# Sample attention: fetching the value pages from GpSimd's queue instead of the sync engine's

## What is computed

```python
k_past = cache_k[i][page_table].reshape(bs, past, SB_HEADS, SB_HEAD_DIM)
v_past = cache_v[i][page_table].reshape(bs, past, SB_HEADS, SB_HEAD_DIM)
...
z = jnp.einsum('bqhd,bkhd->bhqk', qblk, k) * scale + bias
log_1mb = jnp.where(mask, jax.nn.log_sigmoid(-z), 0.0)
after = lax.cumsum(log_1mb, axis=3, reverse=True) - log_1mb
w = jnp.where(mask, jnp.exp(jax.nn.log_sigmoid(z) + after), 0.0)
out = jnp.einsum('bhqk,bkhd->bqhd', w, v)
```

## Time and profile before

| | |
|---|---|
| median of three runs | 1210.35 us (1209.7 to 1211.05) |
| span of the profiled execution, first to last instruction | 1205.7 us |
| TensorE busy | 1054.1 us, 87% |
| VectorE, ACT, GpSimd busy | 679.0, 419.7, 32.6 us |
| data moved by DMA | 190.26 MB, 158 GB/s in the mean |
| sample attention, first L1576 to last L1616 | about 371.6 to 533 us |

### The profile page before, as it was taken

One profiled execution on the slowest core, in us unless ns is written; L12 is line 12 of the kernel. 1 busy time (PEld: TensorE's weight loads), 2 busy tenths in 40 slices (PEclk: granted clock), 3 DMA queues, 4 the chain that ended last, 5 costly groups with the idle time before them and its releaser, 6 DMA issues.

```text
span 1205.7 us, 14021 instructions
## 1 busy us (share of the span) xinstructions
PE 1054.1 (87%) x4920; PEld 787.6 (65%) x4920; DVE 679.0 (56%) x1299; ACT 419.7 (35%) x610; POOL 32.6 (3%) x70
## 2 busy tenths in 40 slices
PE   5999999999796576657999679999999999998694
PEld 3576766776453343335667578888888888886573
DVE  2249980111355443336241468998998998987313
ACT  1111111331232232224001255666656666554212
POOL 3000004000000000000010000000000000000000
PEclk9899999999587799967999689999999999999797
DMA  7034256240605366770232246767757777664001
GB/s 210 29 112 140 99 180 206 70 140 3 207 9 159 122 218 226 239 271 21 81 118 91 70 141 220 267 238 263 266 213 248 244 262 261 239 225 160 1 1 43
DMA packets 89128, 190.26 MB, mean 158 GB/s; under 512 B 8201, under 2 KB 8521, under 8 KB 89063
## 3 DMA queue, kind: packets, MB, share of 16 engines
q1 hardware_dynamic: 83520, 183.09, 44.0%
q0 software_dynamic: 1968, 5.65, 1.5%
q10 hardware_dynamic: 3583, 0.80, 0.4%
HBM read 184.23 MB, written 5.64 MB: 157 GB/s over the span
## 4 chain that ended last, share of the span: by engine, by line
PE 53%; DVE 6%; SPq 5%; issue 3%; ACT 2%; DMA 2%; DVEq 0%; POOL 0%; ACTq 0%; POOLq 0%
PE bank L1756 7%; PE bank L1734 7%; PE bank L1758 7%; PE bank L1757 7%; PE bank L1679 4%; PE bank L1852 3%; PE bank L1691 3%; SPq L304 3%; SPq L307 2%; PE bank L1750 2%; PE bank L1751 1%; PE bank L1610 1%; PE bank L1356 1%; DVE scratch L865 1%; DMA out_ssm_sample<-ring 1%
## 5 line engine op out<-in xcount | busy, mean ns | idle before, releaser
L1401 PE MATMUL bank<-scratch,ring 128*128 128x320 f32 x896 | 242.5, 433 | 0.0
L1401 PEld LDWEIGHTS bank<-scratch,ring 128*128 128x128 f32 x896 | 169.8, 190 | 70.6 <-issue 0.5
L1232 DVE TENSOR_TENSOR pieces<-ring,pieces 128x1024 fp32r<-128x1024 f32 x144 | 172.9, 1220 | 15.8 <-ACT pieces L533 10.8
L533 ACT ACTIVATE pieces<-ring 128x1024 fp32r<-128x1024 f32 x144 | 150.4, 1058 | 36.4 <-PE bank L1758 32.2
L533 ACT ACTIVATE proj<-bank 128x320 f32<-128x320 f32 (+4 forms) x91 | 44.0, 492 | 201.2 <-PE bank L1401 117.1
L1734 PE MATMUL bank<-gates 128*128 128x128 f32 x768 | 90.6, 279 | 2.3 <-DVE gates L1223 2.3
L1734 PEld LDWEIGHTS bank<-gates 128*128 128x128 f32 x768 | 89.1, 196 | 2.4 <-issue 2.4
L1756 PE MATMUL bank<-pieces,h_exp 128*128 128x512 f32 x192 | 74.8, 390 | 1.4 <-DVE h_lo L1239 1.4
L1757 PE MATMUL bank<-pieces,h_exp 128*128 128x512 f32 x192 | 74.7, 389 | 0.0
L1758 PE MATMUL bank<-pieces,h_lo 128*128 128x512 f32 x192 | 74.7, 389 | 0.0
L924 DVE SCALAR_TENSOR_TENSOR proj<-scratch,par_w,proj 128x256 f32<-128x256 f32 x240 | 73.7, 380 | 1.1
(11 more groups left out here) (334 smaller groups left out, 1600.8 us busy)
## 6 DMA issues: line engine op xcount, KB each, us to landing
ring<-in_w_expert_gate SPq DMA_DIRECT2D x16, 2048.0 KB, 8.7
ring<-in_w_expert_up SPq DMA_DIRECT2D x16, 2048.0 KB, 8.8
ring<-in_w_expert_down SPq DMA_DIRECT2D x16, 2048.0 KB, 8.4
ring<-in_w_in SPq DMA_DIRECT2D x14, 2048.0 KB, 7.9
ring<-in_cache_k SPq DMA_DIRECT2D x64, 256.0 KB, 4.0
ring<-in_cache_v SPq DMA_DIRECT2D x64, 256.0 KB, 3.9
ring<-in_w_branch SPq DMA_DIRECT2D x3, 2048.0 KB, 10.0
ring<-in_w_out SPq DMA_DIRECT2D x2, 2048.0 KB, 11.1
```

Of the source, the lines that this page charges most:

```text
L533: return F(out, in_, ACT.Copy)
L1232: TT(piece_of[r % 4][:, 1, :], raw_piece(EXPERTS + 3 * e, r), piece_of[r % 4][:, 0, :].bitcast(F32), ALU.subtract).then_inc(s("lo_ready"), 1)
L1401: m = MM(bank[t % 4][:, 0:T], slot(j, DC, GROUP)[:, k, (t % 4) * P:(t % 4 + 1) * P], h[:, k, :], start=k == 0, stop=k == DC - 1)
```

## The change

A common `fetch` for any issuing engine stands ahead of the engines' programs. SP fetches key pages only. All value pages are fetched by GpSimd, in its program order between its stores; SP's wait for `slot3_stored` and all of its `o_done` waits ahead of value pages are gone from its stream. `slot2_stored` is gone: GpSimd itself waits for its stores. The value pages of the last pair go to slots 0 and 1 as before, but are counted on `v_loaded`, and GpSimd waits for the arrival of the value pages before them. Sizes, slots and the work of TensorE, VectorE and ACT stay as they were.

```diff
+        def fetch(eng, which, u, i, to):
+
+            dst = slot(to, NPAGE, W)
+            regs = [eng.value_load(pages[0:1, bass.ds(i * (2 * NPAGE) + (u * NPAGE + p), 1)], min_val=0, max_val=POOL - 1)
+                    for p in range(NPAGE)]
+            for p in range(NPAGE):
+                eng.dma_start(dst[:, p, :], a["cache_" + which][0][bass.ds(regs[p], 1)].rearrange("n s h d -> (n s) (h d)")
+                              ).then_inc(s(f"{which}_loaded{u}"), 16)
...
             sp.wait_ge(s("pages_loaded"), 16)
 
-            def fetch(which, u, i, first=None):
-
-                dst = slot(u + ({"k": 0, "v": 2}[which] if first is None else first), NPAGE, W)
-                regs = [sp.value_load(pages[0:1, bass.ds(i * (2 * NPAGE) + (u * NPAGE + p), 1)], min_val=0, max_val=POOL - 1)
-                        for p in range(NPAGE)]
-                for p in range(NPAGE):
-                    sp.dma_start(dst[:, p, :], a["cache_" + which][0][bass.ds(regs[p], 1)].rearrange("n s h d -> (n s) (h d)")
-                                 ).then_inc(s(f"{'k' if first == 0 else which}_loaded{u}"), 16)
-
             def fetch_k(i):
+
                 for u in range(2):
-                    sp.wait_ge(s("k_page_turned"), i * 16 + (4 * u - 4))
-                    fetch("k", u, i)
-
-            def fetch_v(i):
-                sp.wait_ge(s("o_done"), i)
-                for u in range(2):
-                    fetch("v", u, i)
+                    if i is not 0:
+                        sp.wait_ge(s("k_page_turned"), i * 16 + (4 * u - 4))
+                    fetch(sp, "k", u, i, u)
 
             sp.wait_ge(s("proj_done"), 56)
-            for u in range(2):
-                fetch("k", u, 0)
-            for u in range(2):
-                sp.wait_ge(s(f"slot{2 + u}_stored"), 1)
-                fetch("v", u, 0)
+            fetch_k(0)
             fetch_k(1)
             with sp.Fori(1, NB // 2 - 1) as i:
                 fetch_k(i + 1)
-                fetch_v(i)
-            for u in range(2):
-                sp.wait_ge(s("k_page_turned"), 8 * NB + 4 * u - 4)
-                fetch("v", u, NB // 2 - 1, first=0)
...
             pool.wait_ge(s("stored"), 16 * store.n)
-            pool.sem_inc(s("slot2_stored"), 1)
+            pool.wait_ge(s("pages_loaded"), 16)
+            fetch(pool, "v", 0, 0, 2)
             pool.wait_ge(s("prompt_state_ready"), 1)
             store(o["ssm_prompt"][0, 0].rearrange("(c e) p n -> (e p) c n", e=2), prompt_state)
             pool.wait_ge(s("states_new"), 2)
             store(o["ssm_sample"][0].rearrange("b (c e) p n -> (e p) b c n", e=2), states)
             pool.wait_ge(s("stored"), 16 * store.n)
             pool.sem_inc(s("slot3_stored"), 1)
+            fetch(pool, "v", 1, 0, 3)
+            with pool.Fori(1, NB // 2 - 1) as i:
+                pool.wait_ge(s("o_done"), i)
+                for u in range(2):
+                    fetch(pool, "v", u, i, 2 + u)
+            for u in range(2):
+                pool.wait_ge(s("k_page_turned"), 8 * NB + 4 * u - 4)
+                pool.wait_ge(s(f"v_loaded{u}"), 128 * (NB // 2 - 1))
+                fetch(pool, "v", u, NB // 2 - 1, u)
...
                 for u in range(2):
-                    if first:
-                        pe.wait_ge(s(f"v_loaded{u}"), i * 128 + 128)
-                    else:
-                        pe.wait_ge(s(f"k_loaded{u}"), (NB // 2 + 1) * 128)
+                    pe.wait_ge(s(f"v_loaded{u}"), i * 128 + 128)
```

## The result

The changed kernel takes 1213.19 us (median of 16 runs, 1210.12 to 1214.86), the kernel before on the same chip 1210.03 us (16 runs, 1207.58 to 1211.47). The ratio is 1.0027, with a 95% interval of 1.0019 to 1.0035: **slower by 0.27%, some 3.2 us**. The forecast was 1206.7, faster by 3.7. Of the kernel before, one of the 15 executions beside e9 to e11 was a slow one (1607.67 us at a granted clock of 0.64), and their ratios go by the others.

The account below looks back on a forecast made before the run. TensorE was busy 87% of the span, so only its idle time could be won: 4.8 us from pair 3's key wait less 1.1 for GpSimd's value chain gave 3.7, 1210.35 to 1206.65 us; range 1205.0 to 1214.5.

Parts of the forecast that it names:

- pair 1: TensorE's waits of 6.62 and 4.9 us for pair 1's key pages (L1576): both stay, gain taken as 0.
- pair 3: TensorE's 4.26 us wait for pair 3's key pages goes once SP issues no value pages; gain at most 4.8 us.
- the value chain on GpSimd: From `o_done` through loads, issues and landing to L1610: 26.0 us on GpSimd against 23.3 on SP, pairs 1 and 2.
- The running ahead: GpSimd's sequencer starts second-batch loads while first-batch descriptors are written: pitch 0.375 us, -1.1 us; none had 18% chance.
- The cover: Time from `o_done` until TensorE takes the value pages, 25.4 us; on SP 2.1 us more than the chain.
- value pages become the bound: Rival, 25%, slower: GpSimd's value chain delays L1610 in turns 2 and 3; 1215.8 halfway, 1220.8 us at full size.
- the sign that I had named: L1610 of turns 2 and 3 released by DMA of value pages, with 0.5 to 1 us more idle.
- the 1.1 us which I charged for two turns: GpSimd's value chain exceeds its cover by 0.6 us in turns 2 and 3, costing 1.1 to 1.2 us.
- the early pages: Sequence 0's first value pages move into the input projection, cost 0; a 5% rival shared with the last pair: +3 us.
- the last pair's: Last pair's value pages on GpSimd done at 515, wanted at 519: cost 0, up to +2 us; shared 5% rival.
- the branch loads: SP's two 2 MB branch loads start about 503, beside the last value pages; weights wanted after the prompt's attention: 0.
- the rest of the change: Early pages, last pair, branch loads and added `v_loaded` wait: taken as 0, GpSimd's next work lying after the merge.

Follow-up runs that it names:

- e9: e8 with GpSimd's drain at the end of the program left out; 1193.18 us, ratio 0.9877 to the kernel before.
- e11: The kernel before with GpSimd's drain at the end of the program left out; 1206.70 us, ratio 0.9982.
- e8: The kernel before, all pages on SP, with page numbers loaded ahead of the waits; 1197.11 us, ratio 0.9891.
- e6: The kernel before with only pair 1's value pages (16 DMAs) moved to GpSimd; 1206.51 us, ratio 0.9977.
- e5: The kernel before, unchanged, profiled once more; 1207.27 us in one run.
- e2: The changed kernel with GpSimd's drain at the end of the program left out; 1204.59 us, ratio 0.9964 to the kernel before.
- e1: The changed kernel with one GpSimd drain added right behind its last value-page fetch; 1204.91 us, ratio 0.9965 to the kernel before.
- e3: The kernel before plus 64 idle GpSimd DMAs of one number for each of 128 partitions; 1216.65 us, ratio 1.0054.
- e4: As e3, but each of the 64 idle DMAs touches 16 partitions; 1215.54 us in one run.
- e7: e1 with SP's register loads of key page numbers put ahead of the slot waits; 1202.49 us, ratio 0.9943 to the kernel before.

## Why the prediction was wrong

**Right: pair 1.** "Gain 0 to 0.2 us; I take 0. These two waits stay": they did, 7.43 and 5.13 us after 6.62 and 4.96, and SP's first issue came at 389.33 against 388.88. I took them to be slot turn-round (what lies between a freed slot and its next pages) made of turn, loads, issues and landing; e8, which takes the loads out of it and has the value pages ahead of it out of the way, cut them to 3.15 and 1.91.

**Right in kind, too large: pair 3.** The key wait of 4.26 us went. The price of 4.8 us came out as 3.1 in the profile of after (turn 3, from value matmul to value matmul, 38.2 and 35.1 us) and 3.0 in e6. Before itself varies here: its turn 3 is 39.5 us in e5 and 39.4 in e11, with key waits of 5.04 and 4.79, and against the mean of the three the gain is 3.9. I took turn 2 of before, 33.4 us, as what turn 3 would become, 4.8 less. Turn 3 begins at a lower clock instead: from its first L1576 to its first L1585 it is 482.37 - 475.02 = 7.35 us, not the 5.64 of turn 2 in before. Windows of after (columns as the earlier trace rows; the clock stands before the DMA share):

```profile
406.00:416.00 10.00, 7.42 (x26) 4.68 (x28) 5.10 (x5) 1.20 (x2) 0.00 (x0) 0.53 0.08 33
...
440.00:450.00 10.00, 8.19 (x46) 6.14 (x48) 7.96 (x16) 4.28 (x6) 4.31 (x8) 0.83 0.77 249
...
475.00:485.00 10.00, 7.95 (x46) 6.21 (x47) 7.63 (x16) 4.26 (x6) 4.31 (x8) 0.83 0.64 212
```

In before these three windows have 0.85, 1.00 and 0.83. In 406 to 416 that is mostly the lower of the two levels, 1.2 GHz, behind the two long key waits, and the matmuls of L1585 at 412.22 take 5.96 us instead of 3.65. This is part of the 1.7 us by which turn 1 grew. e2 has the same 5.96; e1 does not, and its turn 1 is as long, because its second key wait is (6.30 us). Which turns begin slowly differs between kernels: turn 2 is 34.7 us in after and e2, 33.5 in e1, 33.4 in e6 and before. By the means of before, e5 and e11 on one side and after, e1 and e2 on the other, turn 1 grew by 1.4 us and turn 2 by 0.9, neither of which my sum had as such, and turn 3 shrank by 3.9. Why all three kernels with the full transfer have the longer turn 1 stays open. e3 and e4 have it too (59.3 and 59.0), with all fetches on SP and GpSimd's idle DMAs beside pair 1's key fetch; e6, where GpSimd issues nothing there, doesn't (57.4), nor do e5 (57.5) and e11 (58.0). So DMAs from GpSimd beside that fetch are the likely cause, but no run was made for it.

**Wrong in size, without harm: the value chain on GpSimd.** The register load, bounded by 0.27 and 0.55 us and taken as 0.49, is 0.29 (line L273 on GpSimd's queue, 430 to 475, min/median/max ns):

```profile
L273 POOLq TENSOR_LOAD <-pages x21: 283/290/310, 437.0 to 474.3; - x21
```

Its issue takes 539 ns, with 4.63 us for eight, and both batches show it (GpSimd's timeline):

```profile
204.59 4.65 POOL L276 DMA_DIRECT2D ring<-in_cache_v  x8 [6.67 <-issue]
...
380.99 4.68 POOL L276 DMA_DIRECT2D ring<-in_cache_v  x8 [14.11 <-issue]
442.92 4.63 POOL L276 DMA_DIRECT2D ring<-in_cache_v  x8 [57.26 <-issue]
452.65 4.63 POOL L276 DMA_DIRECT2D ring<-in_cache_v  x8 [5.10 <-issue]
```

The running ahead that I took for the first batch hardly happened: its eight issues come 0.585 us apart, and the second batch's loads start with the last of them, at 447.0. Against SP's chain of 23.3 us: the first issue comes 6.0 us after `o_done` (ACT's copy, at 436.91), where SP took 6.2; from the first issue to the last, at 456.7, it is 13.8 us, not 12.9; and the landing is 4.4 us, not 4.2. That is 24.2 us, 0.9 more than on SP, where I had 2.7 more. The cover is 463.65 - 436.91 = 26.7. So value pages weren't late in after, and the rival "value pages become the bound" needed terms that the chip doesn't have. But part of that cover came from the slow start of turn 2 in this profile. In e1, whose turn 2 is 33.5 us, the cover is 460.96 - 435.42 = 25.5, and there the value pages did land last, if only by 0.1 us, which is the sign that I had named:

```profile
460.96 7.09 PE L1608 MATMUL bank<-ring,scratch 128*64 128x512 f32 x32 [1.10 <-DMA ring<-in_cache_v]
```

Against the 1.1 us which I charged for two turns that is next to nothing. The register work of eight loads takes 5.4 and 5.0 us in the two batches on GpSimd (436.9 to 442.3, 447.0 to 452.0) and the same on SP in before (435.3 to 440.7, 444.9 to 449.9), where I had +3.9 for the 16; the issues take +1.0 by their pitch, 0.585 for 0.51, where I had +0.4 and, for running ahead, -1.1. So the two mistakes partly hid each other. The page of after has a median landing of 4.4 us for value pages from GpSimd and 4.2 for key pages from SP. The Trainium skill (DMA: Bandwidth & Descriptors, Specifications) sets the two apart by 0.4 us; the 0.2 seen here has that sign and half that size. No wait of TensorE names the early pages, the last pair's or the branch loads in after, as predicted; whether the early move has a part in the longer turn 1 is the question left open above.

**The step that failed: the rest of the change.** "GpSimd's next work lies after the merge" ended my list of what follows on GpSimd. It counted what waits for GpSimd's instructions and left out that the program's end waits for GpSimd itself. The drain of 0.193 us in the earlier trace rows, which I used as a hint on its sequencer, was one with no DMA ahead of it; the other one, 2.356 us at 1203.1, was in the same trace, at the very end of the span. Of a step that is moved to another queue I had priced the issue, the registers and the landing, but not what the queue has to do at the end for each DMA it had issued: I had that at nothing, and it measured 7.586 - 2.356 = 5.2 us, all of it on the path (e2, e11). With the gain that e2 and e11 measure, 5.2 - 2.2 = 3.0 us slower, and 3.2 was measured. Had I known the drain, my own sum would have given 5.2 - 3.7 = 1.5 us slower. The measured time lay within my range only thanks to a rival which didn't happen.

## What to carry to other kernels

When work moves to another queue, look at the end of the program as well: which engine's closing drain ends last, and what makes it long. Here one drain in GpSimd's idle time turned a loss of 0.27% into a gain of 0.35%. And before a fetch is spread over two queues, look at what stands between the free buffer and the first issue: reading the page numbers ahead of the wait was worth 13 us on one queue, while the second queue, which shares the DMA engines, brought about 2, or about 4 in the attention where only the fetch that stood in the way was moved (e6).

## What the hardware showed that I hadn't expected

- GpSimd's drain takes 0.301 us for 3 DMAs since the drain before, 2.356 for 28, 3.666 for 44 (e6) and 7.586 for 92. From 28 to 92 that is 5.230 / 64 = 0.082 us for each DMA, with 0.06 left over; the same line gives 3.67 for 44 and 0.31 for 3. (The drain with no DMA ahead of it, 0.193 us in the earlier trace rows, isn't on this line.) It doesn't depend on rows (e4) or on how long ago they landed (e3).
- Register loads on GpSimd take 0.29 us, near SP's 0.27 and not ACT's 0.49 or VectorE's 0.55.
- Two queues fetching at once took the landing of a 256 KB page from 4.0 to 6.8 us in the median, at 385 GB/s (e7).
